# Last down-projection tile in three pieces (288, 160 and 128 tokens) in place of two of 288

## The reference

```python
def run_layer(x, c, pos, mixer, w_ada, b_ada, ...):
    ada = jax.nn.silu(c) @ w_ada + b_ada
    sh1, sc1, gt1, sh2, sc2, gt2 = jnp.split(ada, 6, axis=-1)
    h = modulate(rms_norm(x, g_pre_mix), sh1, sc1)
    qa, ka, va, qi, ki, wi, qb, kb, vb, ga, gb = project(h, pos, w_in)
    oa, ob = mixer(qa, ka, va, qi, ki, wi, qb, kb, vb)      # top-k attention and differential attention
    m = jax.nn.sigmoid(ga) * (oa @ w_o_a) + jax.nn.sigmoid(gb) * (ob @ w_o_b)
    x = x + gt1[:, None] * rms_norm(m @ w_out, g_post_mix)
    h = modulate(rms_norm(x, g_pre_ffn), sh2, sc2)
    f = (jax.nn.silu(h @ w_gate) * (h @ w_up)) @ w_down     # 1024 -> 2816 -> 1024
    x = x + gt2[:, None] * rms_norm(f, g_post_ffn)          # mean square over all 1024 features
    return x, (ka, va, ki, kb, vb)
```

## Time and profile before

| | us |
|---|---|
| median of 3 runs | 1014.95 (1014.76 to 1015.82) |
| the profiled execution, its own time | 1013.68 |
| its span in the trace | 1011.5 |
| PE busy | 959.1 (95% of the span) |
| PE weight loads busy | 911.6 (90%) |
| DVE busy | 438.3 (43%) |
| ACT busy | 410.6 (41%) |
| POOL busy | 365.2 (36%) |
| DMA | 111.61 MB, mean 110 GB/s |

### The profile page before, as it was taken

One profiled execution on the slowest core, in us unless ns is written; L12 is line 12 of the kernel. 1 busy time (PEld: TensorE's weight loads), 2 busy tenths in 40 slices (PEclk: granted clock), 3 DMA queues, 4 the chain that ended last, 5 costly groups with the idle time before them and its releaser, 6 DMA issues. The chain is left out here.

```text
span 1011.5 us, 17736 instructions
## 1 busy us (share of the span) xinstructions
PE 959.1 (95%) x7104; PEld 911.6 (90%) x7104; DVE 438.3 (43%) x875; ACT 410.6 (41%) x767; POOL 365.2 (36%) x174
## 2 busy tenths in 40 slices
PE   4898999999999989999999899999999999999995
PEld 1687899999998989988888799999999999999995
DVE  5766558988884323333100753333333333000005
ACT  4764335465556455443433842222223222312221
POOL 2031016446353231234454044444444342444440
PEclk9999999999999999999999999999999999999998
DMA  9821022332230113357856022222222212222212
GB/s 365 323 87 47 7 84 87 108 104 85 72 119 34 42 55 128 111 226 255 308 199 198 1 85 85 82 85 80 83 83 83 83 62 81 91 87 86 72 45 94
DMA packets 35600, 111.61 MB, mean 110 GB/s; under 512 B 4240, under 2 KB 9360, under 8 KB 35280
## 3 DMA queue, kind: packets, MB, share of 16 engines
q1 hardware_dynamic: 31152, 102.48, 29.6%
q10 hardware_dynamic: 4112, 6.93, 1.8%
q0 software_dynamic: 272, 1.31, 0.3%
HBM read 100.38 MB, written 10.32 MB: 109 GB/s over the span
## 5 line engine op out<-in xcount | busy, mean ns | idle before, releaser
L1094 POOL TENSOR_TENSOR wlo<-raw,whi 128x1024 fp32r<-128x1024 f32 x52 | 128.8, 2477 | 240.6 <-ACT whi L735 231.2
L1149 POOL TENSOR_TENSOR wlo<-raw,whi 128x1024 fp32r<-128x1024 f32 x41 | 104.7, 2554 | 151.2 <-ACT whi L1057 151.2
L1854 PE MATMUL pj<-hh,wlo 128*128 128x288 f32 (+1 forms) x640 | 137.3, 296 | 0.0
L1854 PE MATMUL pj<-hh,whi 128*128 128x288 f32 (+1 forms) x640 | 137.0, 295 | 0.0
L1854 PE MATMUL pj<-hl,whi 128*128 128x288 f32 (+1 forms) x640 | 136.8, 295 | 0.0
L1617 PE MATMUL pj<-hh,whi 128*128 128x288 f32 x544 | 124.6, 311 | 4.6 <-POOL wlo L1094 2.4
L1617 PE MATMUL pj<-hh,wlo 128*128 128x288 f32 x544 | 117.4, 298 | 0.0
L1617 PE MATMUL pj<-hl,whi 128*128 128x288 f32 x544 | 117.0, 297 | 0.0
L1854 PEld LDWEIGHTS pj<-hh,wlo 128*128 128x128 f32 x640 | 103.4, 189 | 0.0
L1854 PEld LDWEIGHTS pj<-hh,whi 128*128 128x128 f32 x640 | 102.9, 188 | 0.0
L1854 PEld LDWEIGHTS pj<-hl,whi 128*128 128x128 f32 x640 | 102.8, 188 | 0.0
(11 more groups left out here) (224 smaller groups left out, 2000.5 us busy)
## 6 DMA issues: line engine op xcount, KB each, us to landing
raw<-in_w_s SPq DMA_DIRECT2D x94, 512.0 KB, 3.5
rawa<-in_w_ada SPq DMA_DIRECT2D x32, 512.0 KB, 6.2
rawd<-in_w_d SPq DMA_DIRECT2D x16, 704.0 KB, 4.0
raw<-in_w_ada SPq DMA_DIRECT2D x16, 512.0 KB, 10.3
g_raw<-gz ACTq DMA_DIRECT2D x16, 288.0 KB, 2.1
gate<-g_raw SPq DMA_DIRECT2D x8, 576.0 KB, 3.8
rawv<-in_w_v SPq DMA_DIRECT2D x8, 324.0 KB, 4.9
xt<-in_xT SPq DMA_DIRECT2D x2, 1152.0 KB, 7.0
```

The lines of the kernel that those rows point to most:

```text
L1094: pool.tensor_tensor(rest, raw_of(c), whole.bitcast(F32), ALU.subtract).then_inc(w_lo, 1)
L1149: pool.tensor_tensor(wlo[:, slot(c), :], raw[:, raw_slot(c), :], whi[:, slot(c), :].bitcast(F32), ALU.subtract).then_inc(w_lo, 1)
L1854: ins = mm(pj[tile % 2][:, h, 0:HALF + 2 * h], w[:, slot(C_GU + q), b:b + P], x[h][:, kc, :], start=(kc == 0 and w is whi and x is hh2), s ...
```

## The change: three pieces, each with its own accumulator, sum, root, residual and output

A table `PIECES` takes the place of the two halves in the last tile: tokens 0 to 287, 288 to 447 and 448 to 575 (288, 160 and 128 of them). The first two accumulate where the halves did, in the two banks of the last `pj` tile; the third in the first bank of `lg`. Their sums of squares go to the two banks of the next `pj` tile and to `tb`. PE does 22 blocks of three matmuls for each piece, and five blocks into the second and into the third piece it puts in the sum of the piece before. ACT, DVE and SP do for three pieces what they did for two halves, with the piece's width.

```diff
+        last, s3 = pj[(T_DN + KC - 1) % 2], pj[tile_of["stat3"] % 2]
+        PIECES = ((0, HALF, last[:, 0, 0:HALF], s3[:, 0, 0:HALF]),
+                  (HALF, T - P, last[:, 1, 0:HALF - P], s3[:, 1, 0:HALF - P]),
+                  (T - P, T, lg[:, 0, 0:P], tb[:, 0:P]))
...
-            for h in range(2):
+            for h, (c0, c1, _, _) in enumerate(PIECES):
                 for i in range(KC // 2):
                     sp.wait_ge(x2_ready, KC // 2 * h + i + 1)
                     for kc in (2 * i, 2 * i + 1):
-                        sp.dma_start(o["yT"][kc][:, h * HALF:(h + 1) * HALF], x1[:, kc, h * HALF:(h + 1) * HALF])\
-                            .then_inc(y_out, 16)
-            sp.wait_ge(y_out, 16 * 2 * KC)
+                        sp.dma_start(o["yT"][kc][:, c0:c1], x1[:, kc, c0:c1]).then_inc(y_out, 16)
+            sp.wait_ge(y_out, 16 * len(PIECES) * KC)
...
-            def last_tile(n, d, h):
+            def last_tile(d, h):
+                c0, c1, bank, s_bank = PIECES[h]
                 act.wait_ge(last_full, h + 1)
-                act.activation(sq2[:, d, h * HALF:(h + 1) * HALF], pj[n % 2][:, h, 0:HALF], ACT.Square)\
-                   .then_inc(ysq_ready, 1)
-                gained(ymix, 1, n, d, h).then_inc(last_out, 1)
+                act.activation(sq2[:, d, c0:c1], bank, ACT.Square).then_inc(ysq_ready, 1)
+                for w, a0, a1 in HALF_SPANS[0] if h == 0 else ((0, c0, c1),):
+                    ins = act.activation(ymix[:, d, a0:a1], bank[:, a0 - c0:a1 - c0], ACT.Copy, scale=gg[:, 1, d, w:w + 1])
+                ins.then_inc(last_out, 1)
                 act.wait_ge(stat3_full, h + 1)
-                act.activation(rms3[:, h * HALF:(h + 1) * HALF], pj[tile_of["stat3"] % 2][:, h, 0:HALF], ACT.Sqrt,
-                               bias=eps[:, 0:1], scale=1.0 / D).then_inc(rms3_ready, 1)
+                act.activation(rms3[:, c0:c1], s_bank, ACT.Sqrt, bias=eps[:, 0:1], scale=1.0 / D).then_inc(rms3_ready, 1)
...
-            for h in range(2):
-                c0, c1 = h * HALF, (h + 1) * HALF
+            for h, (c0, c1, _, _) in enumerate(PIECES):
                 v.wait_ge(rms3_ready, h + 1)
                 v.reciprocal(rstd3[:, c0:c1], rms3[:, c0:c1]).then_inc(rstd_ready, 1)
                 v.wait_ge(rstd_ready, 6 + h)
                 v.wait_ge(last_out, h + 1)
-                r2 = rstd3[:, c0:c1].unsqueeze(1).to_broadcast([P, 2, HALF])
+                r2 = rstd3[:, c0:c1].unsqueeze(1).to_broadcast([P, 2, c1 - c0])
...
-            def down_block(tile, k, b, h):
+            def down_block(k, b, h):
                 kc = BLK_DOWN * k + b
+                c0, c1, bank, _ = PIECES[h]
                 for w, x in ((dhi, fh), (dhi, fl), (dlo, fh)):
-                    ins = mm(pj[tile % 2][:, h, 0:HALF], w[k][:, b * P:(b + 1) * P], x[:, kc, h * HALF:(h + 1) * HALF],
-                             start=(kc == 0 and w is dhi and x is fh), stop=(kc == FC - 1 and w is dlo))
+                    ins = mm(bank, w[k][:, b * P:(b + 1) * P], x[:, kc, c0:c1], start=(kc == 0 and w is dhi and x is fh),
+                             stop=(kc == FC - 1 and w is dlo))
...
-            for h in range(2):
+            pj_free(pe, T_DN + KC - 1)
+            for h in range(len(PIECES)):
                 for k in range(2):
                     if h == 0:
                         pe.wait_ge(w_lo, lo_count(C_DN + 2 * (KC - 1) + k))
                     for b in range(BLK_DOWN):
-                        ins = down_block(tile, k, b, h)
-                        if h == 1 and (k, b) == (0, 4):
-                            pj_free(pe, tile_of["stat3"])
-                            stat3(0)
+                        ins = down_block(k, b, h)
+                        if h and (k, b) == (0, 4):
+                            if h == 1:
+                                pj_free(pe, tile_of["stat3"])
+                            stat3(h - 1)
                 ins.then_inc(last_full, 1)
-            stat3(1)
+            stat3(len(PIECES) - 1)
```

More of the change, by code:

```diff
@@ L1074, in _ @@
                 f_tile(T_DN + d, d)
-            for h in range(2):
-                last_tile(T_DN + KC - 1, KC - 1, h)
+            for h in range(len(PIECES)):
+                last_tile(KC - 1, h)
         @block.gpsimd
@@ L1860, in _ @@
                 gu(i, 4, 3)
-            def down_block(tile, k, b, h):
+            def down_block(k, b, h):
                 kc = BLK_DOWN * k + b
+                c0, c1, bank, _ = PIECES[h]
                 for w, x in ((dhi, fh), (dhi, fl), (dlo, fh)):
-                    ins = mm(pj[tile % 2][:, h, 0:HALF], w[k][:, b * P:(b + 1) * P], x[:, kc, h * HALF:(h + 1) * HALF],
-                             start=(kc == 0 and w is dhi and x is fh), stop=(kc == FC - 1 and w is dlo))
+                    ins = mm(bank, w[k][:, b * P:(b + 1) * P], x[:, kc, c0:c1], start=(kc == 0 and w is dhi and x is fh),
+                             stop=(kc == FC - 1 and w is dlo))
                 return ins
             def stat3(h):
+                c0, c1, _, s_bank = PIECES[h]
                 for i, (x, sem_, n) in enumerate(((acc2[:, :], acc_ready, N_SUM0 + KC - 1),
@@ L1874, in stat3 @@
                     pe.wait_ge(sem_, n)
-                    ins = mm(pj[tile_of["stat3"] % 2][:, h, 0:HALF], ones[:, :], x[:, h * HALF:(h + 1) * HALF],
-                             start=(i == 0), stop=(i == 1))
+                    ins = mm(s_bank, ones[:, :], x[:, c0:c1], start=(i == 0), stop=(i == 1))
                 ins.then_inc(stat3_full, 1)
@@ L1896, in _ @@
                     ins.then_inc(pj_full if k else down_used, 1)
-            tile = T_DN + KC - 1
-            pj_free(pe, tile)
-            for h in range(2):
+            pj_free(pe, T_DN + KC - 1)
+            for h in range(len(PIECES)):
                 for k in range(2):
```

## The result

The changed kernel takes 1018.65 us (median of 15 runs, 1016.45 to 1020.61) against 1015.82 for the kernel before, run beside it; the ratio is 1.0035, 95% interval 1.0025 to 1.0044. The direction is as forecast. The size is not: 2.8 to 3.6 us in place of 19.5, outside the range of 1029 to 1039, and within 0.4 us of the second rival's 1019.0. Two of the fifteen runs of the kernel before took 3598 and 4621 us; without them its median is 1015.49, and the difference of the medians 3.2 us.

A forecast was written before the change was run, and what follows sets the result against it. PE's projection matmuls were taken to bound the last tile until its last sum, then the tail. 31.1 - 8.7 + 0.53 - 3.45 made the end 19.5 us later, forecast 1034.4 us, range 1029 to 1039.

The forecast's parts named there:

- second rival: PE, last tile: narrow matmuls at 0.104 to 0.132 us, together 15.6 us; 1019.0 us in all; chance 0.08.
- the upper price: PE, last tile: narrow matmuls at 0.263 and 0.208 us, together 31.1 us; chance 0.82.
- The row nearest in width: Profile row of 128-column fp32 matmuls, twelve records in 1.25 us, two per matmul: 0.208 us each, taken for narrow fp32r matmuls.
- the floor at one record's pace: PE, last tile: one record per narrow matmul, 0.104 to 0.132 us, from weight load or half-rate columns; 15.6 us; chance 0.08.
- The hint from the padded logits: Logits of the 128-key block are computed over 256 columns, 128 read; waste if narrow fp32r matmuls cost by the column.
- By the column, the first rival,: PE, last tile: matmuls at 0.075 and 0.061 us, DVE's serial work eats the gain; +0.2 us, 1015.2; chance 0.08.
- The tail: From PE's last sum to the span's end: 12.39 us becomes 8.94, 3.45 saved, with SP becoming the bound.
- What lies beside: First two pieces' ACT, DVE and SP work ends by 1018, so the third finds them idle; extra instructions cost nothing more.

The follow-up runs named there:

- second probe: Kernel before with unread narrow matmul groups added behind the last sum, each after 24 of 384 columns; fp32r with 128 weight columns stood 0.108 to 0.111 us apart.
- experiment 4: Changed kernel with the third piece's matmuls computed over 256 columns, 128 of them used; 1.0028 against the kernel before, 30.4 us in the trace against 29.8.
- experiment 3: Changed kernel with 60 of the 132 narrow matmuls left out; 0.9998 against the kernel before, 26.8 us in the trace.
- first probe: Kernel before with 17 groups of 24 unread matmuls added behind the last sum; 0.217 us apart at granted clock 0.50, 0.114 at 1.00.

## Why the prediction was wrong

- **The step that failed: "I take the upper price. The row nearest in width carries it".** It put a matmul of 160 or 128 columns at 0.263 and 0.208 us, and both took 0.111: the term of 31.1 us for the 132 narrow matmuls measured 14.7 (16.20 less both sums, 0.97 and 0.53). Everything else in the sum held within 0.2 us: with 14.7 in its place the sum is 14.7 - 8.7 + 0.53 - 3.45 = +3.1, against 3.2 in the trace. The width of the range, 1029 to 1039, was my estimate; no row or run shows its ends, and the changed kernel's fifteen runs lie between 1016.45 and 1020.61.
- **Why the row misled.** A row of 128 moving columns also has 128 weight columns. In the second probe an fp32 record of 128 moving columns takes 0.114 even over 32 weight columns, nearly twice the 0.060 of fp32r there, and one of 64 moving columns over 128 weight columns takes 0.108, as much as in fp32r: the row, with 0.104, lies where both lines cross and could not tell them apart. Taking it over to fp32r, I multiplied by two records, and fp32r leaves one.
- **The rival that held: the floor at one record's pace.** It had the mechanism ("from the weight load") and, with 15.6 us, the size, and I gave it 0.08. Its 0.104 was read off fp32 records, which by the crossing above could owe it to either side; fp32r showed the same floor. It took 0.132 for 160 columns, but the floor measured hardly depends on the moving columns (0.108 to 0.111 from 32 to 224); with 0.104 for both the same paragraph had 1017.1, and 0.111 lies between.
- **The hint from the padded logits** counted in the wrong direction (experiment 4). Padding that costs nothing says nothing about what it avoids.
- **By the column, the first rival,** is refuted on PE, but its working of DVE holds: experiment 3 takes away PE's extra time, as that rival would, and it came out at +0.2 in the trace as worked out.
- **The tail** was right in its mechanism, SP becoming the bound included, and by 0.13 us in sum (9.07 against 8.94). One part was off: eight issues at 0.43 each were put at 3.44 and took 3.90, since 0.43 is an issue's length and not the distance to the next, and since SP paused for 0.37; a shorter way from the last issue to the end hid half of it. What lies beside was right too: DVE idle before the second and third reciprocal.

## What to carry to other kernels

In these runs a matmul that loads its weights costs the larger of two times, that of its moving and that of its weight columns; with 128 fp32r weights (0.108 to 0.111 us from 32 to 224 moving columns, 0.118 at 256), cutting the moving side under some 256 columns doubles the loads and saves nothing. Before shortening a tail by cutting its input, see whether the engine behind can take the first pieces sooner: here DVE could not, and cheap cuts would have gained nothing either. And a bound taken from a neighbouring row needs the row's other dimension checked, since a floor and a rate can meet in the very row one reads.

## What the runs showed of the hardware that was not expected

- TensorE's granted clock fell to 0.50 twice in the first probe, while PE issued matmuls without a break: from 1005.3 to about 1025.7, and from 1046.3 to 1063.3. The first time a group of 32 moving columns over 128 weight columns in fp32r had just ended, the second time one in fp32 was under way. The first time the clock stayed low through groups of 64, 128 and 160 columns and most of the 192. In the second probe, with groups of 384 columns in between, it stayed at 1.00, and so it did in the changed kernel through 16 us of 160 and 128 columns. The distance between matmuls of 128 columns doubled with it (0.217 against 0.110).
- DVE's multiplications and POOL's additions, both on SBUF, held each other up. Two of DVE's took 2.3 in place of some 0.80 us, and each ended 0.75 us after one of POOL's had ended; three of POOL's took 2.3 us, the last 1.66 (an addition of 576 elements takes 1.42 with DVE idle, L1128 of the kernel before at 984.83). DVE's reciprocal, which reads one operand, was not held up beside POOL's third addition: 1.54 us for 224 columns, where 6.25 ns a column and the 0.15 that this leaves over at 288 make 1.55.
- Among the last eight transfers of the changed kernel, an issue on SP lasts 0.43 us, but the next one starts 0.47 to 0.49 after it when it has nothing to wait for; the first one and the one behind the pause last 0.33, and the next start 0.37 and 0.38 after them.
